# Prompt attention: another order of the query tiles

## The reference

```python
s = jnp.einsum('bqhd,bkhd->bhqk', qb, k) * scale        # 128 queries, 1024 keys, 8 heads of 96
s = jnp.where(key_pos[None, :] <= q_pos[:, None], s, -jnp.inf)
p = jax.nn.softmax(s, axis=-1)
ctx = jnp.einsum('bhqk,bkc->bqhc', p, ckv_f)
return jnp.einsum('bqhc,chv->bqhv', ctx, w_uv_f)
```

## Time and profile before

| | us |
|---|---|
| three runs | 2164.29, 2164.31, 2165.42 |
| their median | 2164.31 |
| the profiled execution, device time | 2160.58 |
| its span, first to last instruction | 2158.8 |
| mean granted clock of TensorE in it | 0.998 of full |
| the block of prompt attention in it | from 215.5 to 370.1 |

### The profile page before, as it was taken

How to read it: one execution, slowest core, us unless ns; L and a number is a source line. 1 busy time by engine, 2 the same in 40 slices (tenths; PEclk the granted TensorE clock), 3 DMA queues, 4 the chain that set the end, 5 groups by cost and what they waited for, 6 DMA issues and landing times.

```text
span 2158.8 us, 34045 instructions
## 1 busy us (share of the span) xinstructions
PE 2120.2 (98%) x12617; PEld 1779.6 (82%) x12617; DVE 1517.7 (70%) x2364; ACT 969.6 (45%) x2276; POOL 698.1 (32%) x770
## 2 busy tenths in 40 slices
PE   8999998999999999999999999999999999999999
PEld 6988666888787878787878768899999999987776
DVE  4447866888788888888888776677676676754345
ACT  5447665556565655565656553311111211133334
POOL 1754102575656656565657351100000000000000
PEclk9999999999999999999999999999999999999999
DMA  5200101260504041313222133411111111054343
GB/s 185 62 18 1 72 17 39 105 217 8 176 9 157 28 140 45 127 57 111 74 102 94 40 128 108 142 47 41 49 49 48 39 49 49 20 187 160 131 178 128
DMA packets 96532, 185.31 MB, mean 86 GB/s; under 512 B 9496, under 2 KB 65648, under 8 KB 88031
## 3 DMA queue, kind: packets, MB, share of 16 engines
q1 hardware_dynamic: 80797, 99.15, 14.0%
q0 software_dynamic: 15600, 84.40, 11.5%
HBM read 169.49 MB, written 14.36 MB: 85 GB/s over the span
## 4 chain that ended last, share of the span: by engine, by line
PE 79%; DVE 3%; issue 0%; ACT 0%; DMA 0%; DVEq 0%; ACTq 0%
PE ca_banks L2115 32%; PE ca_banks L2797 23%; PE ca_banks L3109 11%; PE ca_banks L2091 5%; PE ca_banks L2183 4%; PE ca_banks L2127 3%; PE ca_banks L3082 0%; DVE ca_cells L2633 0%; DVE ca_cells L2638 0%; DVE ca_lo L2483 0%; PE ca_banks L2232 0%; DVE ca_room L2913 0%; PE ca_banks L2211 0%; DVE ca_down_lo L3170 0%; ACT ca_w_o_hi L2321 0%
## 5 line engine op out<-in xcount | busy, mean ns | idle before, releaser
L2394 ACT ACTIVATE ca_banks<-ca_banks 128x512 f32<-128x512 f32 x512 | 298.2, 582 | 324.3 <-PE ca_banks L2115 320.0
L2115 PE MATMUL ca_banks<-cache_w_hi,ca_hi 128*128 128x512 f32 x1024 | 428.1, 418 | 6.2 <-DVE ca_lo L2483 5.5
L2633 DVE TENSOR_REDUCE ca_cells<-ca_banks 128x8 f32<-128x512 f32 x512 | 352.2, 688 | 88.0 <-ACT ca_banks L2394 72.8
L2115 PE MATMUL ca_banks<-cache_w_lo,ca_hi 128*128 128x512 f32 x1024 | 403.2, 394 | 0.0
L2115 PE MATMUL ca_banks<-cache_w_hi,ca_lo 128*128 128x512 f32 x1024 | 401.6, 392 | 0.0
L2115 PEld LDWEIGHTS ca_banks<-cache_w_hi,ca_lo 128*128 128x128 f32 x1024 | 193.3, 189 | 46.3
L2115 PEld LDWEIGHTS ca_banks<-cache_w_hi,ca_hi 128*128 128x128 f32 x1024 | 193.2, 189 | 44.2 <-DVE ca_lo L2483 10.3
L2115 PEld LDWEIGHTS ca_banks<-cache_w_lo,ca_hi 128*128 128x128 f32 x1024 | 193.9, 189 | 32.2
L1981 POOL TENSOR_TENSOR ca_product<-cache_kpe,attn_q_row_odd 128x512 f32<-128x512 f32 x128 | 164.6, 1290 | 171.5 <-DVE ca_cells L2638 170.1
L2483 DVE TENSOR_TENSOR ca_lo<-ca_banks,ca_hi 128x512 fp32r<-128x512 f32 x256 | 174.9, 683 | 57.1 <-ACT ca_hi L2291 56.6
L1981 POOL TENSOR_TENSOR ca_product<-cache_kpe,ca_q_row_even 128x512 f32<-128x512 f32 x128 | 164.7, 1294 | 131.0 <-DVE ca_cells L2638 129.7
(11 more groups left out here) (466 smaller groups left out, 4257.2 us busy)
## 6 DMA issues: line engine op xcount, KB each, us to landing
ca_down_raw<-in_w_down SPq DMA_DIRECT2D x44, 512.0 KB, 3.3
keep_w_uv<-in_w_gate SPq DMA_DIRECT2D x22, 512.0 KB, 3.9
ca_up_raw<-in_w_up SPq DMA_DIRECT2D x22, 512.0 KB, 3.7
keep_ctx<-in_w_down SPq DMA_DIRECT2D x22, 512.0 KB, 3.9
late_room<-in_x_prompt SPq DMA_DIRECT2D x8, 512.0 KB, 4.3
ca_m<-mixed_scratch SPq DMA_DIRECT2D x8, 512.0 KB, 4.2
ca_w_raw<-in_w_o SPq DMA_DIRECT2D x16, 256.0 KB, 2.6
ca_x<-in_x_prompt SPq DMA_DIRECT2D x8, 512.0 KB, 3.7
```

The lines of the kernel that those rows point to most:

```text
L2115: last = nc.tensor.matmul(KK[:, t, :], x[:, n % 2, t, ck, :], w[:, par, ck, :], start=(m == 0), stop=(m == 5))
L2394: nc.scalar.activation(SQ[:, t, :], KK[:, t, :], ACT.Square).then_inc(squared, 1)
L2633: nc.vector.tensor_reduce(ss[:, par, 2 * n + t, :], SQ[:, t, :].rearrange("p (h d) -> p h d", d=DN), AX.X, ALU.add).then_inc(summed, 1)
```

## The change

The order of query tiles within a pair of heads becomes 0, 7, 1, 6, 2, 5, 3, 4 for the first three pairs, and the same list reversed (4, 3, 5, 2, 6, 1, 7, 0) for the last. Both heads of a pair still follow each other for each tile. With this order no item waits for item 0, since items 0 and 1 share the two banks that item 3 takes and its `before` is 1; so the number of first scores is now found as the first item that waits for any item. It is 3.

```diff
-        items = [(hp, PT - 1 - i if hp % 2 else i, e) for hp in range(NH // 2) for i in range(PT)
-                 for e in range(2)]
+        small_large = [t for i in range(PT // 2) for t in (i, PT - 1 - i)]
+        turns = [small_large] * (NH // 2 - 1) + [small_large[::-1]]
+        items = [(hp, i, e) for hp in range(NH // 2) for i in turns[hp] for e in range(2)]
...
-            issued = before.index(0)
+            issued = next(m for m in range(len(items)) if before[m] >= 0)
```

## The result

| | before | after |
|---|---|---|
| median of six runs each, us | 2164.3 | 2180.7 |
| lowest and highest, us | 2162.6, 2165.4 | 2178.8, 2191.5 |
| ratio of the times, 95% interval | | 1.0084, 1.0071 to 1.0096 |
| the profiled execution: device time, span, us | 2160.6, 2158.8 | 2178.8, 2177.1 |
| prompt attention in it, us | 215.5 to 370.1 | 215.7 to 387.8 |

The change makes the kernel slower: the medians differ by 16.4 us, and the interval of the ratio, in which the longest execution of 2191.5 weighs more, stands for 15 to 21 us. The forecast was +9 us, to 2173: the right direction, and 2180.7 lies inside the range of 2162 to 2184, but the rise is about twice what was worked out.

A forecast was written before the change was run, and what follows sets the result against it. Prompt attention was taken as TensorE-bound for large items, with the new order closing a loop across engines. Terms 2 + 7.7 - 1 gave +8.7, rounded to +9 us: 2173 us, range 2162 to 2184.

The forecast's parts named there:

- the chain: Forward rounds: closed loop through VectorE, ScalarE's copies, large pair's mix and next scores; laps 10.51, 10.08, 9.67, 8.20 us.
- the +7.7: Second and third pairs of heads: loop laps of 38.8 us a pair against 33.3 and 36.6 net before, +7.7 us.
- the first pair: Stage start to end of the mix at item 16: equal to before but for reflection and start clock, +2 us.
- the reflection's two steps: VectorE's reflection steps after items 10 and 14 stand inside the loop and add 1.4 us.
- The start clock's +1: First 5 us of the stage: granted clock 0.75 now meets item 3's scores, +1 us (bounds 0 and 1.9).
- the extras: Decode preparation's small matmuls and the waits before them, in prompt attention: stay at 11 us (bounds -2 and +4).
- rival (D): TensorE's clock dips in each of 12 forward laps, +15 us on top, 2188 us; chance 0.05.
- the last pair: Reversed order, end of the mix at item 48 to stage end: 30.3 us against 31.8, taken as -1 us.
- the 0.5: Excess of a TensorE-bound round over its work in the kernel before, added to 7.9 us for a last-pair round.
- the opening: Last pair, the part ahead of its two rounds, after the mix at item 48: 4.5 us.
- The tail: Last pair, after its two rounds: mix of 9 tiles, 8-tile items' transposes and copies, last mix; 8.7 us.
- rival (A): Levelling works: prompt attention rounds cost 7.9 + 0.5 us, 16 rounds 134, -3 us, 2161 us; chance 0.12.

The follow-up runs named there:

- the two loads on VectorE: Three short extra maxima in each of the first twelve rounds, added to the changed kernel with small steps moved (2173.7): after N(L1) 2178.8 us, after N(s0) 2173.0 us.
- when moved: Changed kernel with decode preparations moved to small items and reflection steps to items 5, 8, 9, 12: 2173.7 us, ratio 1.0045.
- the load outside: Changed kernel with small steps moved, plus three short maxima on VectorE behind the first small item's normalising, where it waits for scores: 2173.0 us, ratio 1.0040.
- ScalarE's order: ScalarE at most one exponential ahead, so copies come earlier: on the changed kernel 2174.3 us, ratio 1.0048; on the kernel before 2165.6 us, ratio 1.0014.

## Why the prediction was right in direction and short in size

**Right: the chain.** The forecast laps were 10.08, 9.67 and 8.20; with nothing threaded in they measure 10.38, 9.99 and 9.17. The first two are 0.3 short each, of which the output copy in front of the large mix is the likely part; the two loads on VectorE show that they are bound as described. The third isn't: there TensorE's own work sets 9.17, where the forecast's 8.20 has neither the whole mix (1.17 us for the large pair's part of 2.39) nor the scores of the first large item. With preparations at small items the two middle pairs take 87.0 us, +6.0 on the kernel before, against the +7.7 of the forecast. The sum hides two errors that cancel: longer laps, and preparations that cost less than their 11 us when they fall into a wait. The second pair takes 41.0 us there, which is its four laps (11.07, 10.74, 9.99 and 9.18 between waiting peaks); the two preparations in the second of them cost 0.4 (10.74 against 10.38 in the first pair). Those of the third pair cost more: its second and third laps take 11.49 and 11.64, 1.1 and 1.7 over the same laps without any.

**Right: the first pair, with a wrong term in it.** +1.5 measured, +2 forecast. Of the reflection's two steps inside the chain only the first shows in the laps: peak to peak 10.93 after, 9.99 when moved, so +0.94; the second came to 0.09 (9.26 against 9.17), since it lies in the lap from 5 to 8 tiles. That leaves 0.6 for the rest, which the forecast took as equal. The start clock's +1 didn't come: the granted clock there was 1.00, not 0.75 as in the earlier trace rows. A clock read off one profile at one place was taken over to another order as if it were fixed.

**Wrong: the extras.** "Half of them now stand behind a large item's copies and half behind a small one's, and I take that as even (bounds -2 and +4)." The measured term is +7.5 us between the items 16 and 48, where nothing but the preparations was moved; the medians give back 7.0 with the reflection moved too. This is the step that failed, and it has two parts. In the new order TensorE is on the chain just where they stand, so the waits in front of them (6.1 us in front of five, 4.0 in the earlier trace rows), the small matmuls and their copies on ScalarE lengthen a lap. That such work costs by its place was said of the reflection, and not applied to the preparations. The two half-clock stretches are the other part: by the rows, 1.30 and 1.25 us for the two rows of scores, and 0.5 for each of the transposes behind them, 3.5 in all, which leaves 4.0 for the places. The laps say the same: the 7.5 us are 2.4 in the second pair, where the clock is full, and 5.1 in the third, where both stretches lie. What isn't shown is that the places of the preparations caused the stretches. The kernel with the load outside has the same places as the one with the steps moved and a median 0.7 us lower, and its profile has 3.4 us at half clock from 336.4 us on, with no wait of TensorE in front.

**Half right: the clock, rival (D).** The forecast had it at a price of 15 us with a dip in each of 12 forward laps. In the profile it comes twice, behind two waits of the third pair, and costs 3.5 us. A loss by the clock is thus a part of the outcome, at a quarter of the rival's size; that the waits bring it on, as the rival has it, isn't shown. The Trainium skill, TensorE: Matmul & The Clock Gate, HAM oscillation, describes a loop throttled by its own idling each time round. The trace agrees only in part: TensorE waits in most forward laps (up to 0.7 us in front of the mix, and five times 1.3 to 1.6 us elsewhere), and ten of twelve keep the full clock.

**Wrong: the last pair.** -1 forecast, +2.6 in both profiles that have it. "I find no loop longer than TensorE's 7.9 plus the 0.5": the rounds take 9.0 (360.76, 369.76, 378.73 above). But that is 1.2 us for the two rounds. The larger error is the opening, which was put at 4.5 and takes 7.35 (353.41 to 360.76): TensorE has 18 tiles of transposes and as many of scores to do in it, 5.8 us by the forecast's own prices, and waits for 0.9. The tail takes 9.0 for 8.7, and the forecast's terms add up to 30.0, not 30.3. Of the +2.6, 1 us is only moved across the cut at item 48, by the run with the last pair alone, whose stage is 1.5 longer. The 0.5 was taken from a round of 8-tile items, where transposes come in long runs. In a mixed round TensorE comes to the next unit before ScalarE has emptied one of two banks. The kernel after, TensorE between two mixes of the last pair:

```profile
366.56 0.52 PE L1525 MATMUL at_T<-keep_ident,at_probs 128*128 128x128 f32 x3 [0.56 <-ACT at_pT L1632]
```

The 8.4 us of a round sank rival (A) as well: 16 rounds of 9.0 to 9.5 us are 144 to 152, where it had 134. The Trainium skill, Perfetto Trace Analysis, Optimization Strategy, holds that interleaving regimes of different bounds may help. No run here shows that: the mixed order with its chain open and its small steps moved is 4.3 us slower than the smooth one (2168.4 against 2164.1), some of which can be the clock's.

**What is shown and what is not.** Shown by runs: the chain (loads inside and outside), ScalarE's order as a step of it (6.4 us, with no gain in the old order), the places of the small steps (7.0 us, the two together 11.1), and that the last pair can't be the cause of more than 3 us. Only read from one profile: the clock's 3.5 us, and the work that fills the lap from 5 to 8 tiles. The runs of the changed kernel had mean granted clocks from 0.990 to 0.998 and times from 2191.5 to 2178.8, the longest time at the lowest clock, so its share may be larger in some executions than in the profiled one. Open: what makes the clock fall where it does, and how much the moved preparations would give in the kernel before at an equal clock.

## What to carry to other kernels

Where each engine's order is written out, evening out the work of rounds says nothing of the time: follow one item through all queues, in the order in which they are written, and see if the walk comes back to its start; the length of that walk is the round. Small work threaded in by item number is part of such a change even where the diff doesn't touch it: look where each piece now falls, and whether the engine is on the walk there or waiting. A round's overhead measured in one mix of sizes doesn't hold for another, since buffers that hide a copy behind eight tiles don't behind three.

## What the runs showed of the hardware that was not expected

TensorE's granted clock fell to half at different places with the order of the work: at the start of the stage in the kernel before (and not after), at 320 and 334 us after (3.4 us each), at 334 us for 10.2 us with every pair reversed and for 6.8 us with the small steps moved as well, at 303 us for 10.2 us in the kernel before with its preparations moved. In the kernel after, both stretches began right behind waits of 1.34 and 1.60 us in front of small matmuls, but such a wait is neither enough nor needed here. Five others of 1.3 to 1.6 us had no fall behind them, and in the reversed order with the small steps moved TensorE hadn't waited for more than 0.3 us in the 3 us before its fall. Scores took twice as long in these stretches (2.50 against 1.25 us), and in the kernel after each cost about 1.8 us.
